# Stick-breaking attention: the values summed by parts, instead of a second sigmoid and a product

## What is computed

```python
def sb_attend(q_pos, q, k, v, k_pos):
    z = jnp.einsum('bhqd,bhkd->bhqk', q.astype(jnp.float32), k.astype(jnp.float32)) * (HEAD_DIM ** -0.5)
    mask = k_pos[None, :] < q_pos[:, None]
    log_skip = jnp.where(mask, jax.nn.log_sigmoid(-z), 0.0)
    later = lax.cumsum(log_skip, axis=3, reverse=True) - log_skip
    w = jnp.where(mask, jnp.exp(jax.nn.log_sigmoid(z) + later), 0.0)
    return jnp.einsum('bhqk,bhkd->bhqd', w, v.astype(jnp.float32)).astype(v.dtype)
```

## Time and profile before

| | |
|---|---|
| median of 3 runs | 1491.63 us (1491.36 to 1492.41) |
| the profiled execution | 1489.05 us, of which the profile's span is 1487.3 us |
| mean granted clock of PE | 0.963 |
| attention stage | 537 to 834.4 us of the span; its stick-breaking half to about 699.5 |
| busy in the whole span | PE 92%, DVE 74%, ACT 50% |

### The profile page before, as it was taken

One profiled execution on the slowest core, in us unless ns is written; L12 is line 12 of the kernel. 1 busy time (PEld: TensorE's weight loads), 2 busy tenths in 40 slices (PEclk: granted clock), 3 DMA queues, 4 the chain that ended last, 5 costly groups with the idle time before them and its releaser, 6 DMA issues. The chain is left out here.

```text
span 1487.3 us, 25707 instructions
## 1 busy us (share of the span) xinstructions
PE 1362.1 (92%) x9697; PEld 1134.1 (76%) x9697; DVE 1103.8 (74%) x1490; ACT 746.2 (50%) x1088; POOL 321.1 (22%) x219
## 2 busy tenths in 40 slices
PE   6959799999999988898999999899869989999985
PEld 4647699999999955566666899788558867888852
DVE  6556758888999968888767354532569979999956
ACT  8512323323433457777777411312247767877733
POOL 0082423223223210000000022021013323333310
PEclk9989899999999999999999999999779999999997
DMA  9335334445455477644750344553478998998566
GB/s 337 121 87 142 87 119 109 127 131 149 141 158 177 135 229 222 219 166 126 214 141 2 100 139 155 177 184 128 170 227 237 301 344 265 283 278 253 125 152 254
DMA packets 219158, 264.30 MB, mean 178 GB/s; under 512 B 92958, under 2 KB 171138, under 8 KB 219028
## 3 DMA queue, kind: packets, MB, share of 16 engines
q1 hardware_dynamic: 209532, 228.06, 48.3%
q0 software_dynamic: 9504, 34.61, 9.7%
HBM read 241.92 MB, written 74.18 MB: 213 GB/s over the span
## 5 line engine op out<-in xcount | busy, mean ns | idle before, releaser
L2492 DVE TENSOR_TENSOR experts_ulo<-plain,experts_uhi 128x2048 fp32r<-128x2048 f32 (+1 forms) x68 | 151.2, 2226 | 19.6 <-ACT experts_uhi L2426 17.6
L594 POOL TENSOR_TENSOR proj_csum<-proj_raw 128x512 f32<-128x512 f32 x80 | 106.8, 1336 | 263.8 <-PE G L776 183.6
L2426 ACT ACTIVATE experts_uhi<-plain 128x2048 fp32r (+1 forms) x68 | 126.4, 1864 | 22.4 <-PEq L78 11.9
L2319 POOL DMA_INDIRECT moe_d<-experts_yo,all_slots x33 | 74.9, 2270 | 205.6 <-DMA moe_d<-experts_yo,all_slots 150.1
L2352 PE MATMUL G<-experts_uhi,experts_ghi 128*128 128x512 f32 x264 | 109.2, 414 | 7.7 <-DVE experts_glo L2497 6.7
L818 ACT ACTIVATE proj_chi<-proj_csum 128x512 fp32r<-128x512 f32 x80 | 50.4, 632 | 113.6 <-POOL proj_csum L594 113.6
L1345 ACT ACTIVATE items_WT<-TB 128x512 f32<-128x512 f32 (+1 forms) x168 | 86.4, 556 | 40.0 <-PE TB L1257 39.5
L2352 PE MATMUL G<-experts_uhi,experts_glo 128*128 128x512 f32 x264 | 105.3, 399 | 0.0
L2352 PE MATMUL G<-experts_ulo,experts_ghi 128*128 128x512 f32 x264 | 105.3, 399 | 0.0
L1391 DVE TENSOR_TENSOR_SCAN items_stick_rows<-items_stick_rows,items_unit 128x512 f32<-128x512 f32 (+3 forms) x104 | 93.7, 943 | 13.0 <-ACT items_stick_rows L1321 10.5
L948 DVE TENSOR_TENSOR proj_clo<-proj_csum,proj_chi 128x512 fp32r<-128x512 f32 x80 | 70.0, 875 | 39.5 <-ACT proj_chi L818 38.4
(11 more groups left out here) (401 smaller groups left out, 3543.7 us busy)
## 6 DMA issues: line engine op xcount, KB each, us to landing
plain<-in_w_dram SPq DMA_DIRECT2D x132, 512.0 KB
plain<-in_w_dram SPq DMA_DIRECT2D x33, 1024.0 KB
ada_raw<-in_w_ada_dram SPq DMA_DIRECT2D x6, 2048.0 KB
proj_raw<-in_w_in_dram SPq DMA_DIRECT2D x20, 512.0 KB
qk_d<-rows SPq DMA_DIRECT2D x16, 576.0 KB, 2.8
gate_d<-rows SPq DMA_DIRECT2D x15, 576.0 KB, 2.8
pre_raw<-in_w_ada_dram SPq DMA_DIRECT2D x32, 256.0 KB, 6.3
out_dram<-proj_tok SPq DMA_DIRECT2D x32, 256.0 KB, 4.5
```

The lines of the kernel that those rows point to most:

```text
L594: pool.tensor_tensor(csum[s % RING], weight(p, a), weight(p, b), op).then_inc(w_sum, 1)
L2319: pool.indirect_dma_start(moe_d, bass.IndirectOffsetOnAxis(ap=dest[:, n:n + 1], axis=0), yo[n % 2][:], None, compute_op=ALU.add).then_inc( ...
L2426: act.activation(half(uhi[j], c)[:, part, :], raw_up(side[n], c)[:, part, :], ACT.Copy).then_inc(u_hi, 1)
L2492: dve.tensor_tensor(half(ulo[j], c)[:, part, :], raw_up(side[n], c)[:, part, :], half(uhi[j], c)[:, part, :].bitcast(F32), ALU.subtract).t ...
```

## The change

- `weigh` and the multiplication stay only for the late step. In the others DVE scans straight into S, and that is what PE turns.
- Each stick-breaking pair gets a tile vs: the value rows shifted by one key, less the value rows. In `values` PE multiplies the turned scan by vs, and adds the value rows of the step's own query block by two products with the identity.
- vs is loaded by two more transfers in `load_v`: partitions 1 to 127 from rows 0 to 126 of each block, and partition 0 from the last row of the block before. DVE clears one row and subtracts vt (`value_steps`), right behind `stick` of the pair's first step; it first waits for all five transfers of `load_v`.
- A bank of z is given back when `remain` is done with it.
- The tile of zeros is half as wide, so each store into moe_d becomes two.

```diff
-                WIDE = SEQ + P
+                WIDE = 512 + P
...
+                vs = [sb(f"vs{j}", [P, TT - 1, P]) for j in both]
...
+                v_loaded = lambda pr: 16 * sum(5 if i < PAIRS else 3 for i in range(pr % 2, pr + 1, 2))
...
                     def load_v(pr):
...
+                        if not f:
+                            old = v_d.rearrange("(t p) n -> p t n", p=P)[:, :, u * P:(u + 1) * P]
+                            sp.dma_start(vs[j][1:P, :, :], old[0:P - 1, 0:TT - 1, :]).then_inc(v_in[j], 16)
+                            sp.dma_start(vs[j][0:1, 1:TT - 1, :], old[P - 1:P, 0:TT - 2, :]).then_inc(v_in[j], 16)
...
-                                sp.dma_start(moe_d[t * P:(t + 1) * P, :], unit[:, 0:D]).then_inc(blank_out, 16)
+                                for c in both:
+                                    sp.dma_start(moe_d[t * P:(t + 1) * P, c * 512:(c + 1) * 512], unit[:, 0:512]).then_inc(blank_out, 16)
...
-                                    pe.wait_ge(s_ready, n_parts[n0] + c0 + 1)
+                                    pe.wait_ge(r_ready, n_parts[n0] + c0 + 1)
...
+                            pe.wait_ge(scanned, 2 * n_parts[n + 1])
...
+                            if pr < PAIRS:
+                                pe.wait_ge(steps_ready, pr + 1)
...
+                        if not fox(n) and not late(n):
+                            for e in both:
+                                pe.matmul(G[side_of[e], 4 + y % 2, (t % 4) * P:(t % 4 + 1) * P], vt[j][:, t, side_of[e]], ident[:],
+                                          start=True, stop=False)
+                            for b in range(nblocks(n)):
+                                for e in both:
+                                    m = pe.matmul(G[side_of[e], 4 + y % 2, (t % 4) * P:(t % 4 + 1) * P], vs[j][:, b, side_of[e]], w[:, 2 * b + e, :],
+                                                  start=False, stop=b == nblocks(n) - 1)
...
                             remain(i + AHEAD, 0)
-                            weigh(i + AHEAD, 0)
+                            if late(i + AHEAD):
+                                weigh(i + AHEAD, 0)
...
+                        dst = late_stick if late(n) else s
+                        if n > AHEAD:
+                            dve.wait_ge(turned, uses[n - AHEAD])
...
-                        dve.tensor_tensor(s[:, :, 0:w], s[:, :, 0:w], SC[:, :, first + 1:SEQ + 1], ALU.mult).then_inc(sb_ready, 1)
...
+                    def value_steps(pr):
+                        j = pr % 2
+                        dve.wait_ge(v_in[j], v_loaded(pr))
+                        dve.memset(vs[j][0:1, 0, :], 0.0).then_inc(row_cleared, 1)
+                        dve.wait_ge(row_cleared, pr + 1)
+                        dve.tensor_tensor(vs[j][:], vs[j][:], vt[j][:, 0:TT - 1, :], ALU.subtract).then_inc(steps_ready, 1)
...
                             stick(i + 1)
+                            if steps[i + 1][1] == 0:
+                                value_steps(steps[i + 1][0])
```

More of the change, by code:

```diff
@@ L999, in stage_items @@
                 S = [sb(f"S{i}", [P, 2, SEQ]) for i in range(AHEAD + 1)]
-                stick_rows = sb("stick_rows", [P, 4 * SEQ + 2])
+                stick_rows = sb("stick_rows", [P, 2 * (SEQ + 2 * P)])
+                vs = [sb(f"vs{j}", [P, TT - 1, P]) for j in both]
                 R = [stick_rows[:, j * SEQ:(j + 1) * SEQ].rearrange("p (e n) -> p e n", e=2) for j in both]
-                SC = stick_rows[:, 2 * SEQ:].rearrange("p (e n) -> p e n", e=2)
+                late_stick = stick_rows[:, 2 * SEQ:].rearrange("p (e n) -> p e n", e=2)
                 fb = [fb0[:], stick_rows[:, 0:2 * (SEQ + 2 * P)].rearrange("p (e n) -> p e n", e=2)]
@@ L1026, in stage_items @@
                 masks = sem("masks")
-                z_ready, s_ready, r_ready, scanned, sb_ready = sem("z_ready"), sem("s_ready"), sem("r_ready"), sem("scanned"), sem("sb_ready")
+                z_ready, s_ready, r_ready, scanned, sb_ready, steps_ready = (
+                    sem("z_ready"), sem("s_ready"), sem("r_ready"), sem("scanned"), sem("sb_ready"), sem("steps_ready"))
+                row_cleared = sem("row_cleared")
                 min_ready, exp_ready, inv_ready, fox_ready = sem("min_ready"), sem("exp_ready"), sem("inv_ready"), sem("fox_ready")
@@ L1060, in stage_items @@
                 slot = lambda n, e: 2 * (n % (AHEAD + 1)) + e
-                QK_DMAS, KC_DMAS, V_DMAS, F_DMAS = 16 * 2, 16 * 3, 16 * 3, 16 * 2 * (2 + NB)
-                FIRST_MASKS = 4
+                QK_DMAS, KC_DMAS, F_DMAS = 16 * 2, 16 * 3, 16 * 2 * (2 + NB)
+                v_loaded = lambda pr: 16 * sum(5 if i < PAIRS else 3 for i in range(pr % 2, pr + 1, 2))
+                FIRST_MASKS = 3
                 MASKS = FIRST_MASKS + 4 + 1 + 2 * 3
@@ L1078, in past_only @@
                                                                 base=0 if f else -1, pattern=[[-1, P]], channel_multiplier=1))
-                    step.inc(pool.memset(unit[:, 0:SEQ], 0.0))
-                    step.inc(pool.tensor_copy(unit[:, SEQ:WIDE], ident[:]))
-                    step.inc(pool.memset(SC[:, :, SEQ:SEQ + 1], 0.0))
+                    step.inc(pool.memset(unit[:, 0:512], 0.0))
+                    step.inc(pool.tensor_copy(unit[:, 512:WIDE], ident[:]))
                     step.inc(pool.memset(qz[0][:], 0.0))
@@ L1170, in _ @@
                             if pr == PAIRS + 1:
-                                sp.wait_ge(sb_ready, N_SB)
+                                sp.wait_ge(sb_ready, PAIRS)
                             if pr >= PAIRS + 2:
@@ L1197, in _ @@
                                 sp.dma_start(raw0[:, j], w[0].rearrange("(k p) n -> p k n", p=P)[:, :, 0:P]).then_inc(early_in, 16)
-                    sp.wait_ge(blank_out, 16 * (TT + 1))
+                    sp.wait_ge(blank_out, 32 * (TT + 1))
                 @block.tensor
@@ L1216, in scores @@
                                 else:
-                                    pe.wait_ge(s_ready, n_parts[n0] + c0 + 1)
+                                    pe.wait_ge(r_ready, n_parts[n0] + c0 + 1)
+                                    if late(n0):
+                                        pe.wait_ge(s_ready, steps[n0][0] + 1)
                             if late(n):
@@ L1246, in turn @@
                             pe.wait_ge(fox_ready, n_fx(n + 1))
+                        elif late(n):
+                            pe.wait_ge(sb_ready, steps[n][0] + 1)
                         else:
-                            pe.wait_ge(sb_ready, n + 1)
+                            pe.wait_ge(scanned, 2 * n_parts[n + 1])
                         squares = [(b, e) for b in range(nblocks(n)) for e in both]
@@ L1263, in values @@
                         if t == 0:
-                            pe.wait_ge(v_in[j], V_DMAS * (pr // 2 + 1))
+                            pe.wait_ge(v_in[j], v_loaded(pr))
+                            if pr < PAIRS:
+                                pe.wait_ge(steps_ready, pr + 1)
                         if t % 4 == 0 and y >= 2:
@@ L1271, in values @@
                         pe.wait_ge(t_taken, uses[n + 1])
-                        if not late(n):
+                        if not fox(n) and not late(n):
[6 more added lines that the diff above has]
+                                                  start=False, stop=b == nblocks(n) - 1)
+                        elif not late(n):
                             for b in range(nblocks(n)):
@@ L1368, in _ @@
                             take(i, (2, 3))
-                        if 0 <= i + AHEAD < N_SB and len(parts(i + AHEAD)) > 1:
-                            weigh(i + AHEAD, 1)
                         if i == EARLY_AT:
@@ L1377, in stick @@
                     def stick(n):
+                        pr, t = steps[n]
                         w, s = keys(n), S[n % (AHEAD + 1)]
-                        first = SEQ - w
-                        if n:
-                            dve.wait_ge(sb_ready, n)
+                        dst = late_stick if late(n) else s
+                        if n > AHEAD:
+                            dve.wait_ge(turned, uses[n - AHEAD])
                         for c, (lo, hi, _) in enumerate(parts(n)):
@@ L1389, in stick @@
                             for e in both:
[L1390 to L1394, removed]
-                        dve.tensor_tensor(s[:, :, 0:w], s[:, :, 0:w], SC[:, :, first + 1:SEQ + 1], ALU.mult).then_inc(sb_ready, 1)
+                                above = 0.0 if top else dst[:, e, hi:hi + 1]
+                                dve.tensor_tensor_scan(dst[:, e, lo:hi][:, ::-1], R[x % 2][:, e, 0:hi - lo][:, ::-1], unmask[:, ::-1],
+                                                       above, ALU.mult, ALU.add).then_inc(scanned, 1)
+                        if late(n):
+                            dve.wait_ge(scanned, 2 * n_parts[n + 1])
+                            dve.wait_ge(s_ready, pr + 1)
```

(3 more changed lines are left out.)

## The result

The changed kernel takes 1569.6 us (median of 4, 1567.44 to 1571.29) against 1491.49; the ratio is 1.0525 (95% interval 1.0506 to 1.0544). Forecast were 1579 us, 1535 to 1625.

A forecast was written before the change was run, and what follows sets the result against it. It took PE to bound the FoX half, with PE and DVE both near their limit in stick-breaking. 55.1 + 14.5 + 14.5 - 3.0 + 6 = 87.1 on 1489.05 gave 1576.2, forecast 1579 us, range 1535 to 1625.

The forecast's parts named there:

- The transfer on one engine: Loads of vs: engines share rows equally by a divisor, so one engine takes all 1,016 packets of the 127 partitions.
- Its price: Each vs load: 29 ns a packet of 512 bytes, 29.5 us on one engine (20.8 to 42), four times.
- the first pair: Start of the attention stage: two vs loads ahead of the first modulation piece, its products done at 627.8, plus 55.1 us.
- The second and third pair: Intervals from one finished modulation piece to the second one after: 55.3 us instead of 40.8, plus 14.5 each.
- The clock: PE restarting at 1.2 GHz after standing still ahead of three modulations: 2 us each, 6 in all (0 to 9).
- That the piece, not vs, is late: Second and third pair: the modulation piece behind vs is waited for, not vs itself, needed some 30 us later.
- To the end: Fourth pair, with no vs behind it: the 45.3 us from 654.24 to 699.5 lose 3.0; FoX half untouched.
- A pair: Computing in a stick-breaking pair: 37 to 39 us against 40.8, a gain of 2.7 (0 to 4).
- the prediction's own floor: Lower end of a stick-breaking pair's time: 33.7 of the FoX pair, 2.8 of modulation and 1.8.
- The first rival: Loads of vs: all 16 engines share the 127 rows, vs costs 1.9 us, kernel 1482 us (1477 to 1491); chance 0.11.
- The second rival: Loads of vs: one engine, but what follows isn't held up, only the start is late; 1510 us; chance 0.02.
- the third: Loads of vs: one engine, packets above 41 ns, as nothing runs beside or SP can't issue; over 1627 us; chance 0.03.

The follow-up runs named there:

- experiment 4: Changed kernel with vs loaded by transfers of 15 and 112 partitions for three pairs, by 127 for the fourth alone; 1507.67 us.
- experiment 5: Changed kernel with vs loaded by 127 partitions for the first pair alone, by 15 and 112 for the other three; 1513.62 us.
- experiment 3: Changed kernel with the 127-partition transfer of vs issued by POOL on its own semaphore instead of by SP; 1563.51 us.
- experiment 6: Changed kernel with vs loaded by 15 and 112 partitions, further without the products of the value rows with the identity; 1477.57 us.
- the padded kernel with the new order: Changed kernel with v_d one row down (vs by 128 partitions), value_steps later, and PE turning chunks 0 and 1, then values, then chunks 2 and 3; 1480.92 us.
- the split in 15 and 112: Changed kernel with the 127 partitions of vs loaded by two transfers, of 15 and 112 partitions; 1488.22 us.

## Why the prediction was right

**The transfer on one engine** held in full, from rows of 1, 8, 9 and 128. With the paces of 127 rows (one engine's) and 122 rows (twice that) they fit equal shares by the largest divisor up to 16; shares rounded up would have given both sixteen engines. The Trainium skill, "DMA: Bandwidth & Descriptors", section "Why a DMA increments its semaphore by 16 and not by 1", says the same, and now runs agree: 122 rows on two engines, 127 on one.

**Its price** was the term that was off: 26.3 us, not 29.5. The 29 ns were the time of one packet from start to end, taken as the pace. Packets overlap, and a lone engine did one every 25.9 ns. It isn't quicker than one of sixteen, which do one every 24.5 ns at full rate. Two transfers stand in the first pair, where the piece was finished at 620.20 instead of the 627.8 of the sum: 47.6 us, not 55.1. The price makes 6.4 of these 7.5 us.

**The second and third pair**: 15.6 and 16.2 us against 14.5 and 14.5, or 16.5 with the clock's 2 us, which were a term of their own in the sum and are inside the measured intervals. The shorter vs takes 3.2 off each, so some 2 to 3 us came in that the sum hadn't. The most of it is issuing: behind its hold SP still needs 6.7 us (658.44 to 665.15) to issue vc, the stores of zeros and a store of modulation results before the piece leaves. The four stores of zeros alone are 3.25, and the prediction had put their issuing at nothing. **The clock**: the three slow runs of products take 3.60, 3.60 and 3.24 us against 1.94, together 4.6 us more, of the 6 in the sum.

**That the piece, not vs, is late** held for the fourth transfer, which experiment 4 shows alone. The first transfer by itself costs only DVE's stop (experiment 5, no wait for a piece); PE waits 20.2 us for the first piece only where the second transfer stands ahead of it too, as the sum had it. My reason, that packets pass in the order of one queue, was too narrow. In the changed kernel SP itself is held and issues the piece late (605.93 against 561.60), and with vs in POOL's queue the pieces are late as well (experiment 3).

**To the end** the span gained 1.1 us, not 3.0: 2.2 in the stage, in line with the pairs, and 1.1 lost behind it, in stages that the change doesn't touch. **A pair** gained 2.0, not 2.7: the identity products take 0.27 us a step on PE instead of 0.22 (0.17 of it is time of the kernel, by experiment 6), and of PE's 1.8 us of waits for chunks 1.2 stayed. The 2.7 didn't agree with the prediction's own floor either: 33.7 + 2.8 + 1.8 = 38.3 leaves 2.5, and two units of modulation are 3.9 us on PE, not 2.8. Nor was 38.3 a floor: the padded kernel with the new order takes 36.9 a pair.

The measured terms are 47.6 + 15.6 + 16.2 - 1.1 = 78.3, the growth of the span, against 87.1. Four times 3.2 us too much for vs, 12.8, were in part made good by the 4 us that the other terms had too little; without that the forecast would have been off by 13 us, still within its range.

**The rivals.** The first rival's 1482 was 6 us too good even for the split in 15 and 112, where its condition holds: some 4 of it in the first pair, which lost 2.6 us where the rival had 1 gained (DVE's late start was not paid back), and 2 in the others. The second rival is excluded by experiment 4, where a transfer that nobody waits for costs 18 to 20 us. Of the third, one condition came true: SP can't issue behind the full engine. It cost nothing more, since the sum already had everything behind vs late; its price above 41 ns is excluded by the 25.9.

## What to carry to other kernels

Before adding a load, look at its outermost count: the engines that share it are a divisor of it, and a shifted tile of 127 rows is the natural way to make that one. Cut it (15 and 112), or shift the data in memory so that 128 rows load. Then ask not only who waits for that load but what is behind it on the engines. And when a change moves the pace from one engine to another, orders that were worth nothing become worth something: 9 us here.

## What was not expected of the hardware

- SP is held while a lone engine works off a long transfer: 26.5 us for issuing the next, tiny one. Issuing the long one from POOL doesn't free it: SP was then held 21.5 us at the stores of zeros.
- A packet's own time is not the pace of an engine: 31.5 ns and 25.9 ns for a lone engine with packets of 512 bytes. The pace of each of sixteen at once was much the same, 24.5 ns.
- After stops of 16 and 20 us the same 64 instructions of PE took 3.60 us at a granted clock of 0.50, against 1.94 at the full clock.
